# Expert weights from the tenth chunk on loaded in 4 MB pairs, into four pairs of ring places, with another end sequence

## The reference, cut to what matters

```python
def expert_block(args):
    xb, e = args
    h = xb @ w_up[e] + b_up[e]                     # w_up[e]: 1024 x 2048 float32, 8 MB
    h_glu = jnp.minimum(h[:, :D_FF], SWIGLU_LIMIT)
    h_lin = jnp.clip(h[:, D_FF:], -SWIGLU_LIMIT, SWIGLU_LIMIT)
    act = h_glu * jax.nn.sigmoid(SWIGLU_ALPHA * h_glu) * (h_lin + 1.0)
    return act @ w_down[e] + b_down[e]             # w_down[e]: 1024 x 1024 float32, 4 MB
...
h = x + mix
h = h + moe(rmsnorm(h, norm_ffn), ...)             # 32 experts, 12 MB each, 403 MB in all
y = rmsnorm(h, norm_final)
```

## Time and profile before

| | us |
|---|---|
| median of 3 runs (1144.1 to 1145.9) | 1145.44 |
| the profiled execution, its whole time | 1145.18 |
| the profiled execution, its span | 1143.3 |
| PE busy | 1095.4 (96%) |
| DMA queue of SP, share of 16 engines | 90.5% |
| granted TensorE clock, mean | 0.99 of 2.4 GHz |

### The profile page before, as it was taken

The page is one execution under the profiler, slowest core; times in us unless marked ns, Lnnn a source line. Parts: engine busy times, 40 slices in busy tenths (PEclk is TensorE's granted clock), DMA queues, the critical chain, the costliest instruction groups (busy, mean ns, idle before and its releaser), DMA issues.

```text
span 1143.3 us, 12351 instructions
## 1 busy us (share of the span) xinstructions
PE 1095.4 (96%) x5258; PEld 456.6 (40%) x5259; DVE 372.3 (33%) x542; ACT 156.0 (14%) x307; POOL 9.0 (1%) x22
## 2 busy tenths in 40 slices
PE   6999996899999999999999999999999999999986
PEld 4888874333333333333333333333333333333322
DVE  1436504233333333333333333333333332233324
ACT  3121114111111111111111111111110111100112
POOL 1000000000000000000000000000000000000001
PEclk9999997999999999999999999999999999999998
DMA  7566553799999999999999999999999999999992
GB/s 246 185 246 256 210 216 151 294 388 423 428 427 428 428 428 427 428 427 428 428 428 427 427 427 429 429 427 427 427 427 429 427 427 427 428 427 427 427 411 96
DMA packets 52724, 431.39 MB, mean 377 GB/s; under 512 B 5494, under 2 KB 24922, under 8 KB 28060
## 3 DMA queue, kind: packets, MB, share of 16 engines
q1 hardware_dynamic: 52236, 430.48, 90.5%
q10 hardware_dynamic: 432, 0.10, 0.0%
HBM read 427.00 MB, written 3.48 MB: 377 GB/s over the span
## 4 chain that ended last, share of the span: by engine, by line
PE 64%; DMA 17%; DVE 1%; issue 0%; POOL 0%; POOLq 0%; SPq 0%; ACT 0%; DVEq 0%
PE bank L1060 34%; PE bank L1079 13%; PE bank L1103 7%; DMA ring_b<-in_w_up 7%; DMA ring_a<-in_w_up 7%; PE bank L1033 4%; DMA ring_a<-in_w_down 3%; PE bank L1071 2%; PE bank L1042 2%; PE bank L1052 1%; PE bank L1110 1%; PE bank L1139 0%; PE bank L1126 0%; POOL st L1011 0%; DVE h_tok L1465 0%
## 5 line engine op out<-in xcount | busy, mean ns | idle before, releaser
L1060 PE MATMUL bank<-ring_a,xs 128*64 128x512 f32 x1376 | 327.9, 603 | 8.0 <-DMA ring_a<-in_w_up 5.9
L1414 DVE TENSOR_TENSOR h_tok<-h_tok,bank 128x1024 f32<-128x1024 f32 (+1 forms) x96 | 116.8, 1217 | 357.6 <-PE bank L1103 346.6
L1060 PEld LDWEIGHTS bank<-ring_a,xs 128*64 128x64 f32 x1376 | 90.6, 137 | 190.4 <-issue 181.0
L1060 PE MATMUL bank<-ring_b,xs 128*64 128x512 f32 x672 | 159.8, 601 | 3.6 <-DMA ring_b<-in_w_up 3.6
L1079 PE MATMUL bank<-ring_a,av 128*64 128x512 f32 x656 | 150.5, 595 | 1.4 <-DMA ring_a<-in_w_down 1.4
L405 PE MATMUL bank<-ring_b 128*128 128x264 f32 x448 | 103.1, 391 | 1.6 <-DVE h_tok L755 1.0
L1103 PE MATMUL bank<-y_rows,spread 64*128 64x512 f32 x372 | 101.9, 624 | 0.3 <-DVE h_tok L1414 0.3
L405 PEld LDWEIGHTS bank<-ring_b 128*128 128x128 f32 x448 | 85.7, 193 | 16.5 <-DVE h_tok L755 1.2
L1060 PEld LDWEIGHTS bank<-ring_b,xs 128*64 128x64 f32 x672 | 43.8, 136 | 92.9 <-issue 87.5
L1079 PEld LDWEIGHTS bank<-ring_a,av 128*64 128x64 f32 x656 | 45.2, 137 | 87.3 <-issue 83.5
L1079 PE MATMUL bank<-ring_b,av 128*64 128x512 f32 x336 | 78.1, 596 | 0.0
(11 more groups left out here) (200 smaller groups left out, 586.4 us busy)
## 6 DMA issues: line engine op xcount, KB each, us to landing
ring_a<-in_w_up SPq DMA_DIRECT2D x86, 2048.0 KB, 28.4
ring_b<-in_w_up SPq DMA_DIRECT2D x42, 2048.0 KB, 30.4
ring_a<-in_w_down SPq DMA_DIRECT2D x41, 2048.0 KB, 29.3
ring_b<-in_w_down SPq DMA_DIRECT2D x21, 2048.0 KB, 29.9
ring_b<-in_w_in SPq DMA_DIRECT2D x14, 1024.0 KB, 5.0
ring_b<-in_w_out SPq DMA_DIRECT2D x4, 1024.0 KB, 5.0
ring_a<-in_w_down SPq DMA_DIRECT2D x4, 1024.0 KB, 30.8
ring_a<-in_state_ret SPq DMA_DIRECT2D x1, 2048.0 KB, 12.3
```

The source lines that it names most:

```text
L1060: mm = pe.matmul(bank[half * CAP:(half + 1) * CAP, H + b, :].rearrange("q (k p) -> q p k", k=4), x, src[:, half * FF + b * 512:half * FF + ...
L1414: tt(rows, rows, bank[0:m, C:C + 2, :], ALU.add).then_inc(comb_added, 1)
```

## The change

- **Layout of the chunks.** The two chunks 0, 1 and 2, 3 of w_up, and the two of w_down, now hold neighbouring bytes for each partition: a pair is 32 KB in one piece per partition (four input rows of w_up, eight of w_down). A single chunk still has rows of 16 KB, taken from such a piece.
- **Pairs.** Chunks 0 to 9 are loaded one by one as before (9 into place 0, 8 into place 8). From chunk 10 on, two chunks are one transfer of 4 MB, into places (1, 2), (3, 4), (5, 6) or (7, 8). Place 0 is not used again but for the overflow path. SP issues the pair (s, s + 1) once PE has used both chunks that it overwrites: `mm_done` at least s - 6. Before, chunk s waited for s - 8 and chunk s + 1 for s - 7. A pair has one `landed`, so PE waits for all of it before its first matmul. There are 90 pairs; chunks 190 and 191 are loaded by columns as before, now with a semaphore for each 1 MB half (`last_in`), and PE waits for the second half only at step j = 4.
- **What follows from the layout.** `turn_x` reads xg with a step of 4 elements (2 before), the norm's weights are turned in four pieces instead of two, b_up is read with a step of 8 (4 before), the up matmuls write PSUM as 64x64x8 (64x128x4 before), and ACT's copy `h_out` puts the two halves of each 128 columns together.
- **End sequence.** The `combine` of expert 30 alternate between two pairs of PSUM banks and wait for the addition before the previous one; `combine_last` of the first half move from j = 1, 3, 5 to j = 1, 4 and behind the loop; the three `weigh` move from DVE to POOL, ahead of POOL's chain for the scale.

```diff
-    w_up_v = w_up[0].rearrange("e (c p k) n -> e c p (k n)", p=P, k=2)
-    w_down_v = w_down[0].rearrange("e (c p k) n -> e c p (k n)", p=P, k=4)
+    w_up_v = w_up[0].rearrange("e (c p k) n -> e c p (k n)", p=P, k=4)
+    w_down_v = w_down[0].rearrange("e (p k) n -> e p (k n)", p=P)
...
+        paired = [s for s in range(RING + 1, LAST - 2, 2)]
+        def slot(s):
+            return s if s < RING else 0 if s == RING else 1 + (s - RING - 1) % (RING - 1)
...
-                for s in (RING, RING - 1, *range(RING + 1, LAST)):
-                    if s >= RING:
-                        sp.wait_ge(mm_done, s - RING + 1)
...
+                for s in paired:
+                    r = slot(s)
+                    sp.wait_ge(mm_done, r + 2 if s < 2 * RING else s - RING + 3)
+                    sp.dma_start(ring_all[:, r:r + 2, :].rearrange("p a n -> p (a n)"), pair_src(stream[s])).then_inc(landed[r], 16)
...
+                for p in range(2):
+                    s = LAST - 2 + p
+                    sp.wait_ge(mm_done, s - RING + 2)
+                    for c in range(2):
+                        sp.dma_start(ring(s)[:, c * 2 * FF:(c + 1) * 2 * FF].rearrange("p (k n) -> p k n", k=4),
+                                     last_src(p, c)).then_inc(last_in[p] if c else landed[slot(s)], 16)
...
-                            pe.wait_ge(landed[s % RING], 16 * (s // RING + 1))
+                            pe.wait_ge(*arrived(s))
...
+                            if j == KT // 2:
+                                pe.wait_ge(last_in[p], 16)
...
-                            if p == 1 and j in (1, 3, 5):
-                                combine_last(0, j // 2)
+                            if p == 1 and j in (1, 4):
+                                combine_last(0, j // 4)
+                    combine_last(0, 2)
...
-                dve.wait_ge(gf_in, 16)
-                dve.wait_ge(comb_added, CT * E + CT)
-                for c in range(CT):
-                    weigh(c).then_inc(fin_weighted, 1)
...
+                pool.wait_ge(gf_in, 16)
+                for c in range(CT):
+                    pool.wait_ge(comb_added, CT * E + c + 1)
+                    pool.tensor_tensor(weighted[c], h_tok[0:n, c, 0:512], g_fin[0:n, 0:512],
+                                       ALU.mult).then_inc(fin_weighted, 1)
```

More of the change, by code:

```diff
@@ L111, in hybrid_layer, with chunk_rows, pair_src @@
         place = {chunk: s for s, chunk in enumerate(stream)}
+        LAST = len(stream)
+        paired = [s for s in range(RING + 1, LAST - 2, 2)]
+        def slot(s):
+            return s if s < RING else 0 if s == RING else 1 + (s - RING - 1) % (RING - 1)
+        uses, arrival = [0] * RING, []
+        for s in range(LAST):
+            if s - 1 in paired:
+                arrival.append(arrival[-1])
+            else:
+                uses[slot(s)] += 1
+                arrival.append((slot(s), 16 * uses[slot(s)]))
+        def chunk_rows(kind, e, j, n):
+            if kind == "u":
+                return w_up_v[e, j // 2][:, j % 2 * 4 * FF:(j % 2 + n) * 4 * FF]
+            return w_down_v[e][:, j * 4 * FF:(j + n) * 4 * FF]
         def chunk_src(chunk):
[L114 to L115 removed]
+            return chunk_rows(*chunk, 1)
+        def pair_src(chunk):
+            return chunk_rows(*chunk, 2)
         def last_src(p, c):
[L118 removed]
+            return w_down[0, E - 1].rearrange("(p k) n -> p k n", k=KT)[:, 4 * c:4 * c + 4, p * 512:(p + 1) * 512]
         with ExitStack() as ph:
@@ L916, in hybrid_layer @@
             gf_in = sem("gf_in")
+            last_in = [sem(f"last_in{p}") for p in range(2)]
             fin_part = sem("fin_part")
@@ L932, in hybrid_layer, with arrived @@
             SUMS = CT * (E + 2)
-            LAST = E * CPR
             def ring(s):
-                r = s % RING
-                return ring_a[:, r, :] if r < FIRST else ring_b[:, r - FIRST, :]
+                return ring_all[:, slot(s), :]
+            def arrived(s):
+                r, count = arrival[s]
+                return landed[r], count
             def ups_done(n):
@@ L945, in landings @@
             def landings(r):
-                return 16 * len(range(r, LAST, RING)) + 16 * (r in (place["d", E - 1, p] % RING for p in range(2)))
+                return 16 * uses[r]
             def greatest_load(eng):
@@ L989, in overflow @@
                     for j in range(CPR):
-                        sp.dma_start(ring(j), w_up_v[e, j] if j < UC else w_down_v[e, j - UC]).then_inc(landed[j], 16)
+                        sp.dma_start(ring(j), chunk_rows("u", e, j, 1) if j < UC else chunk_rows("d", e, j - UC, 1)).then_inc(landed[j], 16)
                 each_overflow(sp, greatest_load(sp), overflow)
@@ L1102, in combine @@
                         at = slice(half * CAP, (half + 1) * CAP)
-                        mm = pe.matmul(bank[0:m, C + half, :], spread[at, n % 2 if isinstance(n, int) else 0, t0:t0 + m],
+                        mm = pe.matmul(bank[0:m, at_bank + half, :], spread[at, n % 2 if isinstance(n, int) else 0, t0:t0 + m],
                                        y_rows[at, :], start=True, stop=True)
```

72 lines of the change are left out of this document (39 added, 33 removed).

## The result

The changed kernel takes 1148.6 us (median of 8 runs, 1146.5 to 1151.0) against 1145.6 for the kernel before; the ratio is 1.0030, with a 95% interval of 1.0019 to 1.0041. A second series gave 1148.65 and 1.0026 (1.0015 to 1.0038). It is slower by 3 us, which is 0.3 us from the predicted 1148.3 and on the predicted side. The profiled execution has a span of 1147.0 us.

What follows compares the result with a forecast made beforehand. Weight transfers were taken to bound the kernel: last landing 1113.65 + 4.1 - 5.6 = 1112.15, p = 0 10.0 later at 1122.15, with the tail 1146.45, plus 1.88 outside the span: 1148.3 us. Range for 8 in 10: 1144.0 to 1152.5.

Steps and rivals of the forecast that it cites:

- Term 1: Start of the stream: pairs wait for their second place, the queue runs dry, and pair (20, 21) lands 4.1 us later.
- the bound below: Start of the stream: the late start costs nothing if the gaps only let the slowest of sixteen engines catch up.
- upper bound for level engines: Start of the stream: the late start costs 6.5 us if the sixteen engines run level.
- Term 2: Middle of the stream: rows of 32 KB save 8.3 ns of fixed cost a row, 5.6 us over 84 pairs.
- Rivals 2 (two packets): Middle of the stream: a 32 KB row is carried as two of 16 KB, saving 0, so 1153.9 us; chance 0.12.
- 3 (less a row): Middle of the stream: a row's fixed cost is smaller, saving 3.7 or 2.4 us, so 1150.2 to 1151.6; chance 0.18.
- Term 3: Behind the last pair's landing: PE's work up to p = 0 takes 10.0 us where it was 5.25, +4.8 us.
- PE is free by then: At the last pair's landing: PE has ended the up pair's work, some 9.9 us, landed 9.7 us or more earlier.
- Term 4: Tail from p = 0 to the span's end: 24.4 us before, 24.3 after, one gain and one loss cancelling.
- Small parts: Stepped transposes, four turns for two and the new PSUM write pattern: counted 0, with 0.5 us as the bound.
- rival 1: Start of the stream: the late start is absorbed, giving 1144.2 us, or 1142 with a larger rate gain; chance 0.2.
- the forecast: Whole kernel: the main case, with late start 3 to 5.5 and row gain 5 to 7 us, spans 1146 to 1150; chance 0.47.

Runs made afterwards that it cites:

- the switch at chunk 34: Against the changed kernel, chunks 10 to 33 were loaded one by one, with pairs only from chunk 34 on: 1146.55 us, ratio 1.0005 to before.

## Why the prediction was right, point by point

**What bounds the kernel** was right: the three terms (start of the stream, rate, work behind the last landing) carry the whole result. In the two traces: 1113.65 + 6.7 - 6.85 = 1113.5, + 9.3 = 1122.8, + 24.2 = 1147.0.

**Term 1, +4.1.** Measured 6.7 in the trace, of which 1.7 are the chance end of the first stage; 5.0 are left, inside the bounds (0 to 6.5). Pair (20, 21) landed 2.6 behind the predicted 289.4, and 0.9 with the chance taken off. But what it costs in the whole is less: without the early pairs the time falls by only 2.1 to 2.4 us. So the bound below, a slowest engine that catches up in the gaps, was half true, and the prediction had it as a rival with 0.2 instead of inside the term. The completions show it: the first completion of (20, 21) came at 290.25 against 281.47 for chunk 21, 8.8 us later (7.1 with the chance taken off, where the prediction's upper bound for level engines was 6.5), and 2.1 of this the last completion did not show, since the lag was 1.7 us instead of 3.8.

**Term 2, -5.6.** Measured -6.85 over the 84 pairs by the landings of the two traces, and 5.0 to 5.6 as the difference to the kernel with 16 KB rows. The 6.85 is too large by luck: in before's trace the lag grew by 1.5 us at chunk 189 itself, so that this landing, the last one counted, came 1.5 us late. The mean of the sixteen completions hangs less on such steps; by it the 84 pairs won 5.9 us (825.7 less 819.8), and the kernel with 16 KB rows needs 825.7 too. The line through 2 and 16 KB rows gave 8.3 ns a row; the runs show about 8. Rivals 2 (two packets) and 3 (less a row) are refuted.

**Term 3, +4.8.** Measured: p = 0 started 9.3 behind the last landing instead of 10.0, so +4.05 (the 5.25 of before begins at that late landing). The size was nearly right, the reason partly wrong. "PE is free by then" was false: PE came to the last pair from the pair before, for which it had also waited, and the sum was nearly the same only because that work (9.9 us) takes about as long as a pair on the queue (9.7). Both numbers stand in the prediction; put against each other they say that PE comes 0.2 us late, not early. That the size held all the same was luck. It mattered for the remedy: splitting the last pair, which the prediction's words call for, brought nothing; splitting fifteen did. The gap of 1.5 us ahead of p = 0 was also taken too long; without a landing to wait for it was 0.9.

**Term 4, tail 24.3.** Measured 24.2. POOL's products took 1.3 us each (1.2 assumed) and were hidden. The later copy of y held the second half nearly as long as the products had.

**Small parts, 0**: the kernel with all pairs undone agrees, within 1.3 us and for all of them together.

**The chances.** The prediction's 0.34 for "within 0.2%" is not the sum of its parts: half of rival 1 (0.10) and a third of the forecast (0.16) are 0.26, and slower than 0.2% would then be 0.64 instead of 0.56.

The 3 us are thus two losses, of 2.1 to 2.4 and 3.7 to 4.1 us, and a gain of 5.0 to 5.9, each by its own kernel. As they stand they sum to 0 to 1.5, where the medians give 3.0. But splitting a pair also gives up its long rows, and so hides a part of the loss: 0.08 us for each of the 15 pairs at the end and, of the 12 at the start, for the six behind (20, 21), together 1.7. That makes 7.5 to 8.2 less 5.0 to 5.9, which is 1.6 to 3.2 and holds the 3.0. The intervals of the single terms are over 1 us wide to each side, so more than this can't be asked of the sum; the loss at the start may also be larger by the 1.1 us that the switch at chunk 34 paid again.

## What to carry to other kernels

Where, as here, the engine that computes and the stream that feeds it are close, a larger transfer is to be counted three times: what its longer rows save in the middle, what the queue loses at the start because a place is freed only in pairs, and how late the consumer runs, since it may begin only at the last byte; the last is carried from transfer to transfer and is paid at the end. In this kernel large transfers belonged in the middle of the stream and small ones at both ends: 51 pairs between singles turned +0.3% into -0.37%. And before a wait is called the cause, look at what the waiting engine was doing when the data landed: the row without a DMA behind it, at 1113.66, told that the last transfer's size was not the point.

## What the runs showed of the hardware that was not expected

- The rate depends on the length of a row even at 8 to 32 KB: 421, 427 and 431 GB/s with rows of 8, 16 and 32 KB at the same count of bytes, and 391 with 2 KB. A row costs about 8 ns, a further transfer 9 ns on each engine.
- The sixteen engines drift apart under a continuous stream, and a landing is the last one's: first and last completion were 0.5 us apart at chunk 9 and 10.0 at chunk 189 of before, 7.0 at the last pair of the changed kernel. Gaps of the queue ahead of pair (18, 19) took 1.8 us of it away. What makes the steps was not tested.
- The same first stage ended up to 2.4 us apart in different executions (chunk 9 issued from 207.1 to 209.5), nearly as much as the whole effect studied. Single traces of two kernels can't be subtracted below that.
- A 128x512 product in float32 takes 1.3 us on POOL and 0.65 on DVE.
